# Conditioning slices of a diffusion block: every slice that is worked out beside other stages goes to VectorE alone, and weight splits stand between pairs of chunks at three layer entries

## The chip, the cores and the metric

The kernel runs on one core of one Trainium2 chip. The metric is the device time in microseconds of one execution; the number quoted for the kernel is the median of several runs.

## The reference

The program is a backbone of four layers (D = 1024) over 256 latent tokens (`x`) and 256 context tokens (`ctx`). Each layer is a token mixer (neighbourhood attention in layers 0 and 3, retention in layer 1, a Conformer convolution module in layer 2) and a convolutional gated feed-forward part. Every one of these eight parts is preceded by an RMS norm whose result is scaled and shifted, and followed by a gated residual; shift, scale and gate come from a conditioning vector, another one for latent than for context tokens:

```python
silu_c, silu_cc = jax.nn.silu(c), jax.nn.silu(c_ctx)[None, :]
for i in range(DEPTH):
    mx = jnp.split((silu_c @ ada_w[i] + ada_b[i])[:, None, :], 6, axis=-1)    # 1024 x 6144 weights
    mc = jnp.split((silu_cc @ ada_w[i] + ada_b[i])[:, None, :], 6, axis=-1)
    hx = rms_norm(xs, norm_mix[i]) * (1 + mx[1]) + mx[0]
    hc = rms_norm(cs, norm_mix[i]) * (1 + mc[1]) + mc[0]
    yx, yc = mixer(hx, hc)                       # attention, retention or convolution
    xs = xs + mx[2] * yx
    hx = rms_norm(xs, norm_ffn[i]) * (1 + mx[4]) + mx[3]
    u, v = jnp.split(hx @ w_up, 2, axis=-1)      # 1024 x 5632
    u = jax.nn.gelu(depthwise_conv(u, w_dw, b_dw))
    xs = xs + mx[5] * ((u * v) @ w_down)         # 2816 x 1024
    # cs the same with mc, except in the last layer
```

## The kernel before, in words

**The large products.** The residual stream `X` lies in SBUF as 8 chunks of 128 features by 512 tokens (256 context, called CT, and 256 latent, called XT). All weights are streamed from memory in 424 groups of 128 x 1024 float32 into four slots (`raw`). To multiply at near float32 precision each group is split: ScalarE rounds it to a high half `Whi` (L1266) and VectorE subtracts that from the raw weights to get the low half `Wlo` (L1680). The activations are split alike into `Hhi` (ScalarE) and `Hlo` (VectorE), and TensorE forms three products for each pair: high by high, low by high, high by low (L748 to L750; L754 to L756 where the tokens stand on the partitions). One group is 24 such products of 512 columns. `split(st)` on both engines splits the group three (`LEAD`) ahead of `st`.

**The order** is written out by hand: each engine has its own program, and semaphores tie them together. `weights_used` counts the groups that TensorE is done with, `lo_split` the split ones, `tile_free` the output tiles that were taken from PSUM, `h_ready` the normed chunks.

**Conditioning.** The 6144 outputs of a layer's conditioning matrix are 48 slices of 128; apart from the first 16, each is a weight block of 128 x 1024 (`cond_w`, three slots, loaded by DMAs that ScalarE issues) that has to be multiplied by each of the two conditioning vectors (`cond`, rows 0 and 1) and summed along its 1024 columns. This is not done on TensorE. It is *hosted*: slices are put between VectorE's instructions of other stages. `weigh(n)` on VectorE is a product with a sum in one instruction (L1704), and `cond_store(n)` (L1715) adds the bias three slices later. For some slices VectorE does both vectors. For the others, which are `shared(n)`, VectorE does the product with row 1, then GpSimd multiplies the block in place by row 0 (`scale_weights`, L608), and ScalarE sums the result (`sum_products`, L1283), after which `reload` fetches the next block. Shared are 12 slices in the q, k and v products of layer 0 (`HOSTED`: so many slices in each quarter of each of six blocks of output columns) and all 99 slices of the feed-forward up-projections of layers 0 to 2, which run 11 laps of four groups with three slices a lap. Six slices (`IN_OUT`) are hosted in the output projection of layer 0, one after each tile, the rest in the down-projections.

**Between parts.** Before each norm the squares of `X` have to be summed: GpSimd does it chunk by chunk as tiles of the residual come (`after_residual`, L600 and L602), ScalarE squares the last chunk, and TensorE sums over the features (`norm_sum`). To have TensorE work meanwhile, the last tiles of a projection are made in halves: first their context half, then the latent half, with the norm of the context half in between (`last_halves`, `norm_halves`). The next part then begins with three tiles together, chunk by chunk as these become ready (`three_tiles`; in layer 3 `by_streams`). At such an entry VectorE scales chunks (L1765), makes their low halves (L1756) and splits the next two or three weight groups, called `following`.

**The convolution module** computes a gate per chunk (ScalarE a sigmoid, L1538, VectorE the product `U`, L2107). 31 taps are then shared among VectorE, ScalarE with GpSimd, and TensorE; TensorE's part (L1161) needs shifted copies of `U`, made by DMAs once `U` is there.

## Time and profile before

| | us |
|---|---|
| median of 3 runs | 2446.84 (2445.07 to 2448.78) |
| the profiled execution | 2448.26 |
| its span, from the first to the last instruction | 2446.1 |
| TensorE (PE) busy in it | 2381.3 |
| VectorE (DVE) busy | 1782.1 |
| ScalarE (ACT) busy | 1025.6 |
| GpSimd (POOL) busy | 657.2 |
| mean granted TensorE clock | 0.993 of full speed |

Busy time is the time in which an engine has an instruction in it. TensorE's instructions overlap, so a busy TensorE can still be paced by something; where it stands still the timeline shows the length of the wait in brackets, with the instruction that ended it.

### The profile page before, as it was taken

How to read it: one execution, taken by the hardware profiler on the slowest of the kernel's cores; microseconds unless marked ns; L12 is line 12 of the kernel's file. 1: busy time of each engine (PE TensorE's matmuls, PEld its weight loads, DVE VectorE, ACT ScalarE, POOL GpSimd, SP SyncE). 2: the span in 40 equal slices, each digit the busy share in tenths (PEclk: the TensorE clock that was granted, in tenths of full speed). 3: DMA queues.
4: the chain of work that ended last, by engine and by line, in shares of the span. 5: the costliest groups of instructions: out<-in, count | busy, mean ns of one | idle time of the engine just before them, and what ended most of it. 6: DMA issues, size and time to landing. Idle time of an engine off the chain costs nothing. (4 is left out here: it accounts for less than half of the span.)

```text
span 2446.1 us, 35542 instructions
## 1 busy us (share of the span) xinstructions
PE 2381.3 (97%) x12398; PEld 1951.9 (80%) x12398; DVE 1782.1 (73%) x2667; ACT 1025.6 (42%) x1557; POOL 657.2 (27%) x445
## 2 busy tenths in 40 slices
PE   8998999999999999999999999999999999998999
PEld 6874688888888878888888888668888887867999
DVE  5777788888974355428988777988988775556774
ACT  4356434443232334314444325554444323555543
POOL 2553433333200030022333225843333224101000
PEclk9999999999999999999999999999999999999999
DMA  8550235446633311223555544523554545312556
GB/s 301 166 187 1 70 117 178 163 160 215 207 101 110 99 67 61 95 95 138 171 175 174 178 152 124 148 79 138 172 174 160 185 159 136 122 44 74 190 184 190
DMA packets 104648, 346.20 MB, mean 142 GB/s; under 512 B 13232, under 2 KB 22896, under 8 KB 104544
## 3 DMA queue, kind: packets, MB, share of 16 engines
q1 hardware_dynamic: 72656, 240.26, 29.4%
q10 hardware_dynamic: 28656, 95.16, 12.0%
q0 software_dynamic: 3232, 9.38, 1.8%
q8 instruction: 68, 1.11, 0.2%
q14 instruction: 36, 0.29, 0.0%
HBM read 334.96 MB, written 1.05 MB: 137 GB/s over the span
## 5 line engine op out<-in xcount | busy, mean ns | idle before, releaser
L1680 DVE TENSOR_TENSOR Wlo<-raw,Whi 128x1024 fp32r<-128x1024 f32 x424 | 637.5, 1504 | 268.6 <-ACT Whi L1266 264.9
L1266 ACT ACTIVATE Whi<-raw 128x1024 fp32r<-128x1024 f32 x424 | 448.4, 1060 | 810.0 <-DMA raw<-in_weights 712.7
L748 PE MATMUL bank<-Hhi,Whi 128*128 128x512 f32 (+1 forms) x2136 | 763.3, 357 | 12.5 <-DVE Hlo L1756 5.4
L749 PE MATMUL bank<-Hlo,Whi 128*128 128x512 f32 (+1 forms) x2136 | 755.8, 354 | 0.0
L750 PE MATMUL bank<-Hhi,Wlo 128*128 128x512 f32 (+1 forms) x2136 | 755.7, 354 | 0.0
L748 PEld LDWEIGHTS bank<-Hhi,Whi 128*128 128x128 f32 x2136 | 404.7, 189 | 78.0 <-issue 12.6
L750 PEld LDWEIGHTS bank<-Hhi,Wlo 128*128 128x128 f32 x2136 | 404.7, 189 | 55.3
L749 PEld LDWEIGHTS bank<-Hlo,Whi 128*128 128x128 f32 x2136 | 404.8, 190 | 55.0
L608 POOL TENSOR_TENSOR cond_w<-cond_w,cond 128x1024 f32<-128x1024 f32 x111 | 270.3, 2435 | 556.8 <-DVE square L1704 510.9
L748 PE MATMUL bank<-Ghi,Whi 128*128 128x512 f32 (+1 forms) x770 | 268.3, 348 | 0.9 <-DVE Wlo L1680 0.9
L749 PE MATMUL bank<-Glo,Whi 128*128 128x512 f32 (+1 forms) x770 | 267.3, 347 | 0.0
L750 PE MATMUL bank<-Ghi,Wlo 128*128 128x512 f32 (+1 forms) x770 | 267.2, 347 | 0.0
L600 POOL TENSOR_TENSOR square<-X 128x512 f32<-128x512 f32 (+1 forms) x51 | 76.7, 1503 | 462.9 <-DVE X L1850 453.0
L1704 DVE SCALAR_TENSOR_TENSOR hb<-cond_w,cond 128x1024 f32<-128x1024 f32 x142 | 196.7, 1385 | 4.8
L754 PE MATMUL bank<-Whi,Hhi 128*128 128x512 f32 x480 | 190.1, 396 | 5.8 <-DVE Wlo L1680 2.3
L756 PE MATMUL bank<-Wlo,Hhi 128*128 128x512 f32 x480 | 188.2, 392 | 0.0
L755 PE MATMUL bank<-Whi,Hlo 128*128 128x512 f32 x480 | 188.1, 392 | 0.0
L748 PEld LDWEIGHTS bank<-Ghi,Whi 128*128 128x128 f32 x770 | 144.3, 187 | 22.8 <-DVE Wlo L1680 0.6
L749 PEld LDWEIGHTS bank<-Glo,Whi 128*128 128x128 f32 x770 | 144.3, 187 | 21.6
L750 PEld LDWEIGHTS bank<-Ghi,Wlo 128*128 128x128 f32 x770 | 144.3, 187 | 21.4
L1604 ACT ACTIVATE hb<-hb 128x512 f32<-128x512 f32 (+1 forms) x88 | 51.0, 579 | 216.7 <-DVE hb L2255 216.7
L1283 ACT ACTIVATE cond_w<-cond_w 128x1024 f32<-128x1024 f32 x111 | 116.7, 1052 | 48.0 <-POOL cond_w L608 41.6
(278 smaller groups left out, 2871.0 us busy)
## 6 DMA issues: line engine op xcount, KB each, us to landing
raw<-in_weights SPq DMA_DIRECT2D x424, 512.0 KB, 3.4
cond_w<-in_ada ACTq DMA_DIRECT2D x176, 512.0 KB, 4.1
ada_raw<-in_ada SPq DMA_DIRECT2D x16, 512.0 KB, 15.0
rel_in<-in_rpb POOLq DMA_DIRECT2D x48, 128.0 KB, 5.8
shifted<-U SPq DMA_DIRECT2D x84, 66.0 KB, 2.1
decay_t<-in_dist POOLq DMA_DIRECT2D x4, 640.0 KB, 4.2
X<-in_x SPq DMA_DIRECT2D x4, 512.0 KB, 5.9
shifted<-U ACTq DMA_DIRECT2D x28, 66.0 KB, 2.1
```

Source lines behind the costliest of these rows:

```text
L600: g.tensor_tensor(square[:, c % 2, tok], X[:, c, tok], X[:, c, tok], ALU.mult).then_inc(sum_step, 1)
L608: g.tensor_tensor(w, w, cond[:, 0, :], ALU.mult).then_inc(cond_scaled, 1)
L748: t.matmul(dst, Whi[:, st.slot, w], hi, start=start, stop=False)
L749: t.matmul(dst, Whi[:, st.slot, w], lo, start=False, stop=False)
L750: return t.matmul(dst, Wlo[:, st.slot, w], hi, start=False, stop=stop)
L754: t.matmul(dst, hi, Whi[:, st.slot, w], start=start, stop=False)
L755: t.matmul(dst, lo, Whi[:, st.slot, w], start=False, stop=False)
L756: return t.matmul(dst, hi, Wlo[:, st.slot, w], start=False, stop=stop)
L1266: a.activation(Whi[:, st.slot, :], raw[:, st.slot, :], ACT.Copy).then_inc(hi_split, 1)
L1283: a.activation(w, w, ACT.Copy, accum_out=cond_sum[:, n % COND_SLOTS, 0:1]).then_inc(cond_summed, 1)
L1680: v.tensor_tensor(Wlo[:, st.slot, :], raw[:, st.slot, :], Whi[:, st.slot, :].bitcast(F32), ALU.subtract)\
L1704: last = v.scalar_tensor_tensor(scratch, w, 1.0, cond[:, r, :], ALU.mult, ALU.mult, accum_out=cond_sum[:, slot, r:r + 1])
```

## The change

- `shared` is gone. VectorE does both products of every slice; GpSimd's product and ScalarE's sum are removed, and `reload` waits for VectorE alone.
- `HOSTED` goes from 18 to 20 slices in the q, k and v products of layer 0 and `IN_OUT` from 6 to 4.
- Entries into layers 1 and 2: VectorE scales chunks 2 and 3 before it splits a weight group, and makes their low halves after it; TensorE begins with the products of chunks 0 and 1 for the first tile alone, before it waits for the group of the second (`early`). Entry into layer 3: each of three groups is split after one pair of chunks.
- Convolution: the sigmoid and the gate of chunk 1 are moved to the end of chunk 0.
- At the start of the program ScalarE makes the high half of chunk 2 before that of a weight group.

```diff
-HOSTED = ((0, 0, 0, 0), (0, 1, 1, 1), (1, 1, 1, 0), (1, 1, 1, 1), (1, 1, 1, 1), (1, 1, 1, 1))
+HOSTED = ((0, 0, 0, 0), (0, 1, 1, 1), (1, 1, 1, 1), (1, 1, 1, 1), (1, 1, 1, 1), (2, 1, 2, 0))
-IN_OUT = 6
+IN_OUT = 4
...
         def weighed(n):
-            return 2 * (n + 1) - shared_before(n + 1)
+            return 2 * (n + 1)
...
-            def scale_weights(n, per=0, i=0):
-
-                pool.wait_ge(cond_weighed, weighed(n) + per * i)
-                w = cond_w[:, n % COND_SLOTS, :]
-                g.tensor_tensor(w, w, cond[:, 0, :], ALU.mult).then_inc(cond_scaled, 1)
...
                 pe.wait_ge(tile_free, index + 2)
+                early = 2 if r % 2 == 0 else 0
+                for k in range(early):
+                    pe.wait_ge(h_ready, ready + k + 1)
+                    three(bank[0][:, CT], steps[0], slice(P * k, P * k + P), Hhi[:, k, CT], Hlo[:, k, CT], k == 0, False)
                 pe.wait_ge(lo_split, steps[1].n + 1)
                 for k in range(C):
                     pe.wait_ge(h_ready, ready + k + 1)
-                    for m in range(2):
+                    for m in range(1 if k < early else 0, 2):
...
-            def sum_products(n, per=0, i=0):
-
-                nth = shared_before(n)
-                act.wait_ge(cond_scaled, nth + 1 + per * i)
-                w = cond_w[:, n % COND_SLOTS, :]
-                a.activation(w, w, ACT.Copy, accum_out=cond_sum[:, n % COND_SLOTS, 0:1]).then_inc(cond_summed, 1)
...
                 square_last(r, XT)
-                high(r, 0, 4, 6)
-                split(following[1])
+                if r == 2 * DEPTH - 2:
+                    split(following[1])
+                    high(r, 0, 4, 6)
+                    split(following[2])
+                else:
+                    high(r, 0, 4, 6)
+                    split(following[1])
                 high(r, 0, 6, C)
...
                     for n, tap in enumerate(pool_taps[c]):
+                        if c == 0 and n == 5:
+                            sigmoid(1)
...
+            first_high(2)
             split(Step(2 - LEAD))
-            first_high(2)
...
-                for q, r in enumerate((1,) if shared(n) else (0, 1)):
+                for q, r in enumerate((0, 1)):
                     if first + q:
-                        dve.wait_ge(cond_weighed, first + q + per * i)
+                        dve.wait_ge(cond_weighed, first + q + 2 * per * i)
...
-                    if c > first:
+                    if c > first and between is None:
                         low(c - 1)
+                if between is not None:
+                    split(between)
+                    low(end - 2)
                 low(end - 1)
...
-                if r % 2 == 0:
+                if r == 2 * DEPTH - 2:
                     split(following[0])
-                    normed_chunks(r, 0, 2, 4)
+                elif r % 2 == 0:
+                    normed_chunks(r, 0, 2, 4, following[0])
...
-                    if c == C - 2:
-                        gate(C - 1)
+                    if c in (0, C - 2):
+                        gate(c + 1)
```

What stands where, word for word, at three places (line numbers are those of each version). First VectorE in the last block of v columns of layer 0, up to the copies of v (`COPY V`); before:

```order
92 L1680 TENSOR_TENSOR Wlo<-raw,Whi 128x1024
93 L1715 TENSOR_TENSOR mod<-cond_sum,bias_ada 128x2
94 L1704 SCALAR_TENSOR_TENSOR hb,cond_sum<-cond_w,cond 128x1024
95 L1680 TENSOR_TENSOR Wlo<-raw,Whi 128x1024
96 L1715 TENSOR_TENSOR mod<-cond_sum,bias_ada 128x2
97 L1704 SCALAR_TENSOR_TENSOR hb,cond_sum<-cond_w,cond 128x1024
98 L1715 TENSOR_TENSOR mod<-cond_sum,bias_ada 128x2
99 L1704 SCALAR_TENSOR_TENSOR hb,cond_sum<-cond_w,cond 128x1024
100 L1715 TENSOR_TENSOR mod<-cond_sum,bias_ada 128x2
101 L1704 SCALAR_TENSOR_TENSOR hb,cond_sum<-cond_w,cond 128x1024
102 L1904 COPY V<-bank 128x512 x2
```

and after:

```order
94 L1656 TENSOR_TENSOR Wlo<-raw,Whi 128x1024
95 L1689 TENSOR_TENSOR mod<-cond_sum,bias_ada 128x2
96 L1680 SCALAR_TENSOR_TENSOR hb,cond_sum<-cond_w,cond 128x1024 x2
97 L1689 TENSOR_TENSOR mod<-cond_sum,bias_ada 128x2
98 L1680 SCALAR_TENSOR_TENSOR hb,cond_sum<-cond_w,cond 128x1024 x2
99 L1656 TENSOR_TENSOR Wlo<-raw,Whi 128x1024
100 L1689 TENSOR_TENSOR mod<-cond_sum,bias_ada 128x2
101 L1680 SCALAR_TENSOR_TENSOR hb,cond_sum<-cond_w,cond 128x1024 x2
102 L1689 TENSOR_TENSOR mod<-cond_sum,bias_ada 128x2
103 L1680 SCALAR_TENSOR_TENSOR hb,cond_sum<-cond_w,cond 128x1024 x2
104 L1689 TENSOR_TENSOR mod<-cond_sum,bias_ada 128x2
105 L1680 SCALAR_TENSOR_TENSOR hb,cond_sum<-cond_w,cond 128x1024 x2
```

Four slices with one product each have become five with two, ten products instead of four.

Then VectorE at the end of the output projection of layer 0, from the fifth tile's residual (`X<-bank,mod,X`) to the halves of the last two tiles; before:

```order
283 L1850 SCALAR_TENSOR_TENSOR X<-bank,mod,X 128x256 x2
284 L1680 TENSOR_TENSOR Wlo<-raw,Whi 128x1024
285 L1715 TENSOR_TENSOR mod<-cond_sum,bias_ada 128x2
286 L1704 SCALAR_TENSOR_TENSOR hb,cond_sum<-cond_w,cond 128x1024 x2
287 L1850 SCALAR_TENSOR_TENSOR X<-bank,mod,X 128x256 x2
288 L1680 TENSOR_TENSOR Wlo<-raw,Whi 128x1024
289 L1715 TENSOR_TENSOR mod<-cond_sum,bias_ada 128x2
290 L1704 SCALAR_TENSOR_TENSOR hb,cond_sum<-cond_w,cond 128x1024 x2
291 L1715 TENSOR_TENSOR mod<-cond_sum,bias_ada 128x2 x3
292 L1842 SCALAR_TENSOR_TENSOR X<-bank,mod,X 128x256 x2
```

and after:

```order
287 L1832 SCALAR_TENSOR_TENSOR X<-bank,mod,X 128x256 x2
288 L1656 TENSOR_TENSOR Wlo<-raw,Whi 128x1024
289 L1832 SCALAR_TENSOR_TENSOR X<-bank,mod,X 128x256 x2
290 L1656 TENSOR_TENSOR Wlo<-raw,Whi 128x1024
291 L1689 TENSOR_TENSOR mod<-cond_sum,bias_ada 128x2 x3
292 L1824 SCALAR_TENSOR_TENSOR X<-bank,mod,X 128x256 x2
```

Two slices, each a store and two products, are gone from between the tiles.

Last VectorE at the entry into layer 1, from the scaling of the first two chunks (`hb<-X,scale,bank`); before:

```order
479 L1765 SCALAR_TENSOR_TENSOR hb<-X,scale,bank 128x256 x2
480 L1756 SCALAR_TENSOR_TENSOR Hlo<-hb,mod,Hhi 128x256 x2
481 L1680 TENSOR_TENSOR Wlo<-raw,Whi 128x1024
482 L1765 SCALAR_TENSOR_TENSOR square<-X,scale,bank 128x256 x2
483 L1756 SCALAR_TENSOR_TENSOR Hlo<-square,mod,Hhi 128x256 x2
```

and after:

```order
488 L1739 SCALAR_TENSOR_TENSOR hb<-X,scale,bank 128x256 x2
489 L1730 SCALAR_TENSOR_TENSOR Hlo<-hb,mod,Hhi 128x256 x2
490 L1739 SCALAR_TENSOR_TENSOR square<-X,scale,bank 128x256 x2
491 L1656 TENSOR_TENSOR Wlo<-raw,Whi 128x1024
492 L1730 SCALAR_TENSOR_TENSOR Hlo<-square,mod,Hhi 128x256 x2
```

The scaling of chunks 2 and 3 has moved ahead of the split.

## Rows read from the trace of the kernel before

**Rows 1.** The page's busy table: busy us, share of the span, instructions.
```profile
PE 2381.3 (97%) x12398; PEld 1951.9 (80%) x12398; DVE 1782.1 (73%) x2667; ACT 1025.6 (42%) x1557; POOL 657.2 (27%) x445
```

**Rows 2.** VectorE by line, 350 to 560 us, then 2260 to 2375; busy, mean | idle before.
```profile
L1680 DVE TENSOR_TENSOR Wlo<-raw,Whi 128x1024 fp32r<-128x1024 f32 x40 | 78.8, 1971 | 4.6 <-ACT Whi L1266 4.6
L1704 DVE SCALAR_TENSOR_TENSOR square<-cond_w,cond 128x1024 f32<-128x1024 f32 x30 | 36.7, 1224 | 1.9
...
L1680 DVE TENSOR_TENSOR Wlo<-raw,Whi 128x1024 fp32r<-128x1024 f32 x40 | 48.8, 1221 | 17.0 <-ACT Whi L1266 17.0
```

**Rows 3.** Timeline of a lap in layer 0, VectorE and GpSimd: start, us, instruction [wait].
```profile
490.65 0.81 DVE L2250 TENSOR_SCALAR hb<-bank,fff 128x512 f32<-128x512 f32 x1 [1.63 <-PE bank L750]
...
496.37 3.01 DVE L1680 TENSOR_TENSOR Wlo<-raw,Whi 128x1024 fp32r<-128x1024 f32 x1
...
501.51 0.81 DVE L2250 TENSOR_SCALAR hb<-bank,fff 128x512 f32<-128x512 f32 x1 [0.19 <-issue]
...
495.89 2.40 POOL L608 TENSOR_TENSOR cond_w<-cond_w,cond 128x1024 f32<-128x1024 f32 x1 [8.57 <-DVE square L1704]
```

**Rows 4.** Timeline of VectorE in layer 0, a slice that it does alone.
```profile
100.12 0.15 DVE L1715 TENSOR_TENSOR mod<-cond_sum,bias_ada 128x2 f32<-128x2 f32 x1
100.31 1.23 DVE L1704 SCALAR_TENSOR_TENSOR hb<-cond_w,cond 128x1024 f32<-128x1024 f32 x1
...
101.57 1.23 DVE L1704 SCALAR_TENSOR_TENSOR hb<-cond_w,cond 128x1024 f32<-128x1024 f32 x1
```

**Rows 5.** VectorE by line, 107.7 to 173.8 us; then the timeline, VectorE and TensorE.
```profile
L1704 DVE SCALAR_TENSOR_TENSOR hb<-cond_w,cond 128x1024 f32<-128x1024 f32 x12 | 19.1, 1593 | 0.4
L1680 DVE TENSOR_TENSOR Wlo<-raw,Whi 128x1024 fp32r<-128x1024 f32 x11 | 15.6, 1417 | 8.6 <-ACT Whi L1266 8.6
L1715 DVE TENSOR_TENSOR mod<-cond_sum,bias_ada 128x2 f32<-128x2 f32 x12 | 10.6, 885 | 0.0
...
173.70 1.28 DVE L1904 COPY V<-bank 128x512 f32<-128x512 f32 x2
...
175.47 1.23 PE L1013 MATMUL bank<-QK 64*128 64x256 f32 x4 [2.58 <-DVEq L1906]
```

**Rows 6.** Stretches: length, busy PE, PEld, DVE, ACT, POOL; clock; DMA share, GB/s.
```profile
171.40:186.00 14.60, 11.57 (x56) 6.91 (x55) 8.69 (x21) 7.30 (x19) 7.28 (x6) 0.77 0.47 142
315.20:333.60 18.40, 12.80 (x75) 12.32 (x74) 13.30 (x30) 5.76 (x12) 5.15 (x6) 0.72 0.28 90
1663.90:1674.60 10.70, 9.36 (x76) 9.00 (x76) 9.38 (x22) 4.50 (x10) 1.44 (x3) 1.00 0.32 100
```

**Rows 7.** Timeline at the end of layer 0's output projection, VectorE and TensorE.
```profile
318.99 0.86 DVE L1842 SCALAR_TENSOR_TENSOR X<-bank,mod,X 128x256 f32<-128x256 f32 x2
...
321.01 1.02 PE L858 MATMUL bank<-one,total 128*128 128x2 f32 x4 [5.60 <-POOL total L602]
```

**Rows 8.** Timeline at the entries into layers 1, 2 and 3.
```profile
696.76 0.35 PE L748 MATMUL bank<-Hhi,Whi 128*128 128x256 f32 x1 [0.70 <-issue]
...
1483.67 0.87 DVE L1765 SCALAR_TENSOR_TENSOR square<-X,scale,bank 128x256 f32<-128x256 f32 x2
...
1483.85 0.36 PE L748 MATMUL bank<-Hhi,Whi 128*128 128x256 f32 x1 [1.53 <-issue]
...
2045.65 0.73 PE L754 MATMUL bank<-Whi,Hhi 128*128 128x512 f32 x1 [2.27 <-DVE Wlo L1680]
...
2055.79 0.58 PE L754 MATMUL bank<-Whi,Hhi 128*128 128x512 f32 x1 [1.90 <-DVE Hlo L1756]
```

**Rows 9.** Timeline at the start of layer 2's up-projection, TensorE and VectorE.
```profile
1695.85 0.50 PE L748 MATMUL bank<-Hhi,Whi 128*128 128x512 f32 x1 [0.66 <-DVE Wlo L1680]
...
1699.75 1.36 DVE L1680 TENSOR_TENSOR Wlo<-raw,Whi 128x1024 fp32r<-128x1024 f32 x1
```

**Rows 10.** Timeline of TensorE in the convolution, at chunk 1's taps.
```profile
1524.34 2.78 PE L1161 MATMUL bank<-shifted,taps_diagonal 128*32 128x512 f32 x24 [1.81 <-DMA shifted<-U]
```

More of the change, by code:

```diff
@@ L80 @@
 PER_LAP = 3
-HOSTED = ((0, 0, 0, 0), (0, 1, 1, 1), (1, 1, 1, 0), (1, 1, 1, 1), (1, 1, 1, 1), (1, 1, 1, 1))
+HOSTED = ((0, 0, 0, 0), (0, 1, 1, 1), (1, 1, 1, 1), (1, 1, 1, 1), (1, 1, 1, 1), (2, 1, 2, 0))
 IN_SLICES = sum(map(sum, HOSTED))
-IN_OUT = 6
+IN_OUT = 4
 IN_MIX = IN_SLICES + IN_OUT
-ALONE = sum(HOSTED[1]) + sum(HOSTED[2])
 V_LATE = 2
@@ L470, in streams @@
             return 2 if tok == ALL else 1
-        def shared(n):
-            return ALONE <= n < IN_SLICES or any(p["hosts"] and p["cond_up"] <= n < p["cond_down"] for p in layers)
-        def shared_before(n):
-            return sum(shared(q) for q in range(n))
         def weighed(n):
-            return 2 * (n + 1) - shared_before(n + 1)
+            return 2 * (n + 1)
         def in_down(layer, group):
@@ L649, in pairs_staged @@
                 pool.wait_ge(rel_ready, 2 * j + 2)
-                if layer == 0:
-                    pool.wait_ge(cond_ready, 2)
-                    for n in range(ALONE, IN_SLICES):
-                        scale_weights(n)
                 h = Heads(layer)
@@ L728, in _ @@
                 after_residual(r + 1, out_tile, norm_tokens(layer, 1))
-                if p["hosts"]:
-                    with pool.Fori(0, FC // 2) as i:
-                        for q in range(PER_LAP):
-                            scale_weights(p["cond_up"] + q, PER_LAP, i)
                 if layer < DEPTH - 1:
@@ L1339, in norm_apply @@
                 square_last(r, XT)
-                high(r, 0, 4, 6)
-                split(following[1])
+                if r == 2 * DEPTH - 2:
[5 more added lines that the diff above has]
+                    split(following[1])
                 high(r, 0, 6, C)
-                for st in following[2:]:
-                    split(st)
                 root_of_norm(r, XT)
@@ L1416, in na @@
                 if layer == 0:
-                    sum_products(IN_SLICES - 1)
                     reload(IN_SLICES - 1, p["cond_end"])
@@ L1531, in conv, with sigmoid @@
                 act.wait_ge(cos_loaded, 32)
+                def sigmoid(c):
+                    act.wait_ge(weights_used, p["mix"] + 2 * c + 2)
+                    a.activation(glu_s[:, c % 2, :], bank[2 * (c % 2) + 1][:, :], ACT.Sigmoid,
+                                 bias=cvb[:, 1, c:c + 1]).then_inc(glu_sigmoid, 1)
                 for c in range(C):
@@ L1536, in conv @@
                         split(steps[0])
-                    act.wait_ge(weights_used, steps[1].n + 1)
-                    a.activation(glu_s[:, k, :], bank[2 * k + 1][:, :], ACT.Sigmoid,
-                                 bias=cvb[:, 1, c:c + 1]).then_inc(glu_sigmoid, 1)
+                    if c != 1:
+                        sigmoid(c)
                     if c == C - 1:
@@ L1711, in cond_store @@
                 earlier = 2 * MODS if k + per >= 2 * MODS else 0
-                dve.wait_ge(cond_weighed, weighed(n) + per * i)
-                if shared(n):
-                    dve.wait_ge(cond_summed, shared_before(n) + 1 + per * i)
+                dve.wait_ge(cond_weighed, weighed(n) + 2 * per * i)
                 v.tensor_tensor(mod_slices[:, bass.ds(k - earlier + per * i, 1), :], cond_sum[:, slot:slot + 1, :],
@@ L1745, in norm_scale, with normed_chunks @@
                 dve.wait_ge(scale_ready, r + 1)
-            def normed_chunks(r, half, first, end):
+            def normed_chunks(r, half, first, end, between=None):
                 layer, part = r // 2, r % 2
@@ L1827, in norm_halves @@
                 normed_chunks(r, 0, 0, 4 if r % 2 else 2)
-                if r % 2 == 0:
+                if r == 2 * DEPTH - 2:
                     split(following[0])
-                    normed_chunks(r, 0, 2, 4)
+                elif r % 2 == 0:
+                    normed_chunks(r, 0, 2, 4, following[0])
                 dve.wait_ge(weights_used, following[1].n + 1)
                 add_half(tiles[-1], bank[6], 1, XT, tile_free)
-                normed_chunks(r, 0, 4, C)
-                split(following[1])
-                for st in following[2:]:
-                    split(st)
+                if r == 2 * DEPTH - 2:
+                    for n in range(1, 4):
+                        normed_chunks(r, 0, 2 * n, 2 * n + 2)
+                        if n < 3:
+                            split(following[n])
+                else:
+                    normed_chunks(r, 0, 4, C)
+                    split(following[1])
                 invert_root(r, XT)
@@ L2114, in conv @@
                         split(steps[0])
-                    gate(c)
+                    if c != 1:
+                        gate(c)
+                    else:
+                        dve.wait_ge(tap_done, taps_before[c])
                     dve.wait_ge(tile_free, FREE0 + p["mix_tile"] + 2 * c + 1)
```

10 lines of the change are left out of this document (1 added, 9 removed).

## The prediction, made before the changed kernel ran

> **What bounds the kernel now.** The page's busy table comes first: TensorE is busy 2381.3 us of a span of 2446.1, so all of its idle time together is 64.8 us, and VectorE is the next engine with 1782.1 [rows 1]. A change to VectorE's work can then do two things: it can become the bound inside a loop, or it can lengthen or shorten one of the few places where TensorE stands still. So the second view is VectorE in time, in a lap of the feed-forward up-projection, and the third is the list of TensorE's stalls in the timeline.
>
> In the up-projection TensorE doesn't wait at all once the loop runs. A lap is four weight tiles. VectorE starts on the output of one at 490.65 and on that of the second next at 501.51, so two take 10.86 us, one 5.43 and a lap 21.7; and once per lap it waits for TensorE, 1.63 us at 490.65 [rows 3]. That wait (and 0.2 of small ones) is the room which VectorE has per lap: about 1.8 us. The grouped rows say what fills the rest: in 210 us, which is 40 weight tiles or 10 laps, 40 low halves take 78.8 us at 1971 ns, and 30 hosted products 36.7 us at 1224 ns. In the last layer, where GpSimd does nothing, the same low half takes 1221 ns [rows 2]. The timeline shows why: GpSimd's product starts at 495.89 and lasts 2.40, to 498.29; the low half that starts at 496.37 lasts 3.01, to 499.38, which is 1.1 after GpSimd is done [rows 3]. The reader is to see that VectorE doesn't run slower beside GpSimd, it stands still until GpSimd's instruction has ended.
>
> **The up-projections (3 x 11 laps).** Removed per lap: three GpSimd products and three ScalarE sums, none on the path. Added: three more VectorE products. What a second product costs is seen in a slice that VectorE does alone: starts at 100.31 and 101.57, so 1.26 us [rows 4]; 3 x 1.26 = 3.8 us a lap. Given back: the low halves, 4 x (1.971 - 1.221) = 3.0 us a lap [rows 2]. Net +0.8 us against 1.8 of room, so VectorE keeps 1.0 us a lap and the loop stays TensorE's: 0 us. If the blocking did not go away, the lap would be 3.8 - 1.8 = 2.0 us longer.
>
> The first lap is different, since VectorE starts it late and has no room yet. In layer 2 TensorE gets its tile at 1695.85 after 0.66 of waiting, and wants the next 5.44 later, at 1701.3; that low half starts at 1699.75 and ends at 1701.1 [rows 9]. One more product stands ahead of it (+1.26; -0.14 of blocking goes), so TensorE waits about 0.9. Layer 1 has the same picture, layer 0 a little more slack: 2 x 0.8 = +1.6 us. From both sides: 0 (a blocked low half of the first lap becomes free) to 3 x 1.26 = 3.8.
>
> That exchange can be read in the Trainium skill too. SBUF — State Buffer, in its section on the two sides, says that VectorE (with two SBUF inputs) and GpSimd share a port pair as an exclusive lock, held for a whole instruction: by that rule the blocking goes entirely with the GpSimd products, and the trace agrees (3.01 against 1.22 us). Perfetto Trace Analysis, under Optimizing Scalar/DVE Operations, says that with a saturated VectorE it may make sense to hand work to other engines; by that alone the added 3.8 us a lap would all be a loss, 33 x 2.0 = 66 us. It is the first rival below.
>
> **The q, k and v products of layer 0.** Twelve slices get a second product (12 x 1.26 = 15.1 us) and two slices move here from the output projection; one takes a store and two products, 0.19 + 2 x 1.26 = 2.7 us [rows 4], so 5.4: +20.5 us on VectorE before the attention starts. Back come the blocked instructions. The store of a finished slice, two columns wide, takes 0.15 us alone [rows 4], but the 12 stores between 107.7 and 173.8 take 10.6 us, so 8.8 of it is blocking. The 12 products there take 19.1 instead of 12 x 1.224 = 14.7 (4.4 us), and the 11 low halves 1417 instead of 1221 ns (2.2 us) [rows 5]. ScalarE's sums also wait for GpSimd and hold back its next high half, for which VectorE waits 8.6 us in all [rows 5]; 7.4 of it should go. Together 22.8, so VectorE ends its slices 2.3 us before its present 173.70, near 171.4, which is about when TensorE's last v product ends. One thing gets later: the third block of columns now hosts four slices, which delays the rows of that block by one slice's 2.7 us; I bound the wait that this gives from 0 to 2.7 and take 0.2, since the rows now come well before TensorE turns them (no wait for them stands there). Now TensorE waits 2.58 us for the copies of v behind that queue, until 175.47 [rows 5]; of this I take back 2.5. The wait is followed by a stretch with a mean granted clock of 0.77 [rows 6]; 14.6 us x 0.23 is 3.4 us lost at most, and as most of the work there is a chain through other engines I take 1.5. Sum -4.0 us, roundly (bounds +1, if VectorE is later rather than earlier, and -6).
>
> **The output projection of layer 0.** This is the largest term. Six slices are hosted there, one a tile, each with instructions blocked by GpSimd's squares, so VectorE falls behind: it adds the first halves of the last tiles only at 318.99, after the last slice; GpSimd's squares follow, and TensorE waits 5.60 us, to 321.01, for the sum of squares [rows 7]. The clock falls too: the stretch 315.2 to 333.6 has a mean of 0.72, while the same stretch in layer 2, which hosts nothing, has 1.00 and takes 10.7 us instead of 18.4 [rows 6]. After the change the last two tiles host nothing, which takes 5.4 us and their blocking from VectorE just before this point; the four earlier slices meet the same blocking as now. VectorE is then waiting for TensorE by the seventh tile. Gain: 18.4 - 10.7 = 7.7, less 0.2 for a rest of GpSimd's lag: -7.5 us (bounds -3 and -8).
>
> **The entries into layers 1, 2 and 3.** TensorE waits there for one low half (0.70 and 1.53 us), and in layer 3 for another (2.27) and for a normed chunk (1.90) [rows 8]. The change puts two scaled chunks (0.87 us [rows 8]) ahead of a low half for which VectorE stands waiting, and gives TensorE six half products before it needs that half. Worth the 0.9 and a little in layer 2, where VectorE really waits: -1.0; -0.7 in layer 1, where the low half itself comes 0.3 later. In layer 3 the third weight tile is split before chunks 4 and 5 instead of after 7, so the 2.27 shrinks to about 1 and the chain behind it moves up; but GpSimd's additions for the bias table there don't move, and block the normed chunks as before: -2.5. Sum -4.2 (bounds -1 and -6).
>
> **The convolution.** The second gate is computed a few microseconds earlier, so that its shifted copies are there when TensorE asks for them; now it waits 1.81 us [rows 10]. But VectorE and ScalarE pace this stage and TensorE would mostly wait a little later instead: -0.3 (bounds 0 and -1.8). The swapped pair on ScalarE at the start of the program is put at nothing: TensorE's next chunks there wait for weights that are still being loaded, and if that cover were gone it is worth under 1 us.
>
> **Sum.** +1.6 - 4.0 - 7.5 - 4.2 - 0.3 = -14.4 us. The profiled execution took 2448.26 (span 2446.1), 1.4 above the median of 2446.84; so 2433.9 for a like execution, 2432.4 for the median.
>
> **Rivals.**
> - VectorE becomes the bound in the up-projections (slower). Place: each of the 33 laps. It decides once the net addition passes the 1.8 us of room. With the full 3.8 it costs 2.0 x 33 = 66 us: 2498. Half of the blocking left (1.5 us a lap more) costs 0.5 x 33 = 16 and eats the gains: 2449. Against it speak the 1221 ns of the last layer and the exact ends beside GpSimd. Chance 0.06.
> - A new wait takes the place of the one in the output projection: GpSimd's own queue of squares is still late, half of the 5.60 stays and the clock falls all the same. Then that term is -3.5 and the time 2436.5. Chance 0.17.
> - VectorE ends the v stage no earlier, and TensorE waits for rows besides: the term of layer 0's attention start is +1 instead of -4: 2437.5. Chance 0.15. With the previous one together, and little at the entries, it is 2443, within the measurement: chance 0.08.
> - The granted clock holds better than I take it for, at all three places: another 4 us, 2428. Chance 0.10.
> - The forecast as it stands: 0.44.
>
> **Numbers.** The range is 2427 to 2441: it holds the forecast, the clock case and the two single rivals, and leaves out the VectorE bound and the sum of failures. About 0.2% (4.9 us) is what a measurement of this kernel can tell from no change. Faster by more: 0.44 + 0.10 + 0.17 + 0.15 = 0.86; within: 0.08 and half of the first rival rounded, 0.09; slower: 0.05.
>
> **What would show it.** In the changed profile the low halves of layers 0 to 2's up-projections should have a mean near 1.22 us, the hosted products twice the number at the same 1.22, and VectorE should still wait about 1 us a lap for TensorE. The wait for GpSimd's sum in layer 0 should be gone and the stretch there near 11 us at a clock of 1; the wait before the attention under 0.5. In layers 1 and 2 one or two waits of about 1 us for a low half stand at the start of the up-projection. The prediction is wrong if TensorE waits for low halves in every lap, or if the 7.5 us come back as a later wait.

## The result, and the profile after

The changed kernel takes 2433.04 us, the median of 4 runs (2429.46 to 2437.48), against 2447.62 for the kernel before (4 runs on the same chip). The ratio is 0.9941, with a 95% interval of 0.9927 to 0.9956, so it is faster by 11 to 18 us. The profiled execution is the fastest of the four: 2429.46, with a span of 2427.6, which is 18.5 below the 2446.1 of before. The 4 us between this trace and the median matter below.

The busy table of the changed kernel, which answers to [rows 1] (busy us, share, instructions):

```profile
PE 2372.9 (98%) x12398; PEld 1944.3 (80%) x12398; DVE 1795.1 (74%) x2889; ACT 906.2 (37%) x1335; POOL 383.2 (16%) x334
```

GpSimd has lost 274 us of work and ScalarE 119, while VectorE, which took over both, has gained only 13. The 111 products that it does more (12 + 99) would be 140 us at 1.26; the rest was time in which it stood blocked (its 424 low halves alone fell from 637.5 to 535.4 us). VectorE by line in the up-projection of layer 0, 340 to 550 us, in answer to [rows 2] (busy, mean ns of one | idle before):

```profile
L1680 DVE SCALAR_TENSOR_TENSOR square<-cond_w,cond 128x1024 f32<-128x1024 f32 x60 | 73.5, 1225 | 4.6
L1656 DVE TENSOR_TENSOR Wlo<-raw,Whi 128x1024 fp32r<-128x1024 f32 x40 | 48.7, 1217 | 0.0
```

Sixty products instead of thirty at the same 1.22 us, and the forty low halves have gone from 1971 to 1217 ns. VectorE's starts on the outputs of a lap, with its wait in brackets, in answer to [rows 3]:

```profile
478.16 0.81 DVE L2235 TENSOR_SCALAR hb<-bank,fff 128x512 f32<-128x512 f32 x1 [1.57 <-PE bank L726]
...
489.56 0.81 DVE L2235 TENSOR_SCALAR hb<-bank,fff 128x512 f32<-128x512 f32 x1
...
499.92 0.81 DVE L2235 TENSOR_SCALAR hb<-bank,fff 128x512 f32<-128x512 f32 x1 [1.57 <-PE bank L726]
```

A lap is still 21.76 us, and VectorE still waits for TensorE once in it. The two stretches of layer 0 that [rows 6] showed at clocks of 0.77 and 0.72 (length, busy PE, PEld, DVE, ACT, POOL; clock; DMA share, GB/s):

```profile
171.40:186.00 14.60, 14.06 (x89) 8.75 (x88) 10.43 (x33) 8.21 (x26) 4.49 (x5) 1.00 0.27 98
...
310.50:321.10 10.60, 9.37 (x75) 8.96 (x74) 7.69 (x20) 4.47 (x10) 1.99 (x3) 1.00 0.30 100
```

Both have the full clock. In the first TensorE hardly stops; the second holds the same 75 matmuls that took 18.40 us before and takes 10.60, like the stretch of layer 2 in [rows 6] (10.70). At the end of the output projection, where it waited 5.60 us for GpSimd's sum [rows 7], the timeline now has

```profile
311.18 0.61 PE L838 MATMUL bank<-one,total 128*128 128x2 f32 x4 [0.53 <-POOL total L592]
```

**Where the time went, stage by stage.** Both programs give TensorE the same 12398 matmuls in the same order (but for a few at the entries), so two traces can be laid side by side: for the matmul of the same number, start after minus start before; the growth of that difference in a stage is what the stage gained or lost. The table does so for the main kernels of this study, in us against the trace of before. The columns: from the program's start to 97 us (the second block of q); the attention start of layer 0 (171 to 185); its output projection's end (311 to 334); the entries into layers 1 (689 to 709), 2 (1477 to 1493) and 3 (2041 to 2087); the first laps of the up-projections of layers 1 and 2; the convolution (1493 to 1626); what follows 2087. The first two rows are two executions of one program: they differ by 4.2 in the first column, 2.3 in the last, 1.0 in the convolution and 0.8 in the first "up1", and by 0.3 at most elsewhere.

```text
kernel               start  attn  outproj  L1    up1   L2    conv  up2   L3    rest
changed              +1.2  -5.9   -7.8   -0.8  +1.3  -1.7  +0.1  +1.1  -4.4  -1.7
changed, again       +5.4  -5.9   -7.8   -0.8  +0.5  -1.4  +1.1  +1.1  -4.4  +0.6
hosting only         +0.8  -5.9   -7.8    0.0  +0.9  -0.3  +0.1  +1.0  -1.2  +1.5
orders only          +5.9  -5.2   -0.5   -0.8   0.0  -1.4  +0.2   0.0  -4.4  -0.5
old spread           +5.6  -5.9   -0.2   -0.8  +1.5  -1.3  -0.5  +1.0  -4.4  -1.7
spread only          +1.1  +5.8   -7.8    0.0   0.0  -0.2  +0.6  +0.1  -3.6  -1.7
up shared            +0.6  -5.9   -7.8   -0.8  +0.1  -1.6  +0.2  -0.2  -4.4  -0.5
slice earlier        -1.2  -5.9   -7.8   -0.8  +0.6  -1.7  -0.5  +1.3  -4.4  +0.3
```

Three columns can be trusted, since they repeat to a tenth of a microsecond: the attention start in the six rows with the hosting (-5.9), the output projection in the six with the new spread (-7.8), the entry into layer 1 in the six with the new orders (-0.8). The first column isn't, and no edit was expected to show there. Nor is the last, where no edit is: it goes from -1.7 to +1.5. Part of it is the clock. Behind the same 2.13 us wait at the entry into the last feed-forward part the clock falls to half in five of the fourteen traces ("changed, again", at 2244.1 us, is one) and not in the others, which costs 1.0 to 1.3 us; the rest comes in the last 60 us of the program.

### The profile page after: what moved, and what is told of

Read it like the earlier page. It is cut to its first block and busy times, and to the rows that moved or that the text cites. A ratio compares the mean times of both kernels' runs of the same rounds, so it can differ in the third digit from the quotient of the medians.

```text
span 2427.6 us, 35365 instructions
## 1 busy us (share of the span) xinstructions
PE 2372.9 (98%) x12398; PEld 1944.3 (80%) x12398; DVE 1795.1 (74%) x2889; ACT 906.2 (37%) x1335; POOL 383.2 (16%) x334
## 5 line engine op out<-in xcount | busy, mean ns | idle before, releaser
L1656 DVE TENSOR_TENSOR Wlo<-raw,Whi 128x1024 fp32r<-128x1024 f32 x424 | 535.4, 1263 | 244.3 <-ACT Whi L1246 240.4
L1680 DVE SCALAR_TENSOR_TENSOR square<-cond_w,cond 128x1024 f32<-128x1024 f32 x198 | 242.5, 1225 | 14.9
L1680 DVE SCALAR_TENSOR_TENSOR hb<-cond_w,cond 128x1024 f32<-128x1024 f32 x154 | 202.7, 1316 | 5.2
L730 PEld LDWEIGHTS bank<-Whi,Hhi 128*128 128x128 f32 x480 | 90.1, 188 | 28.4 <-issue 5.7
```

Of the source, the lines that this page charges most:

```text
L730: t.matmul(dst, hi, Whi[:, st.slot, w], start=start, stop=False)
L1656: v.tensor_tensor(Wlo[:, st.slot, :], raw[:, st.slot, :], Whi[:, st.slot, :].bitcast(F32), ALU.subtract)\
L1680: last = v.scalar_tensor_tensor(scratch, w, 1.0, cond[:, r, :], ALU.mult, ALU.mult, accum_out=cond_sum[:, slot, r:r + 1])
```

## The experiments

Each was compared with the kernel before on the same chip, where that one had medians of 2445.77, 2449.18 and 2448.09 us on the three chips that were used. So ratios are given, and what they come to in us is counted with 2447.

### The parts alone: hosting, and orders

The hosting alone is the changed kernel with these pieces put back as they were:

```diff
-                early = 2 if r % 2 == 0 else 0
-                for k in range(early):
...
+            split(Step(2 - LEAD))
             first_high(2)
-            split(Step(2 - LEAD))
```

and likewise in `norm_halves`, `normed_chunks` and the convolution.

> The changed kernel with the old orders at the layer entries, in the convolution and at the start of the program; the conditioning is hosted on VectorE alone with the new spread (20 and 4 slices). My theory: the terms of the hosting stand alone, +1.6 (first laps of the up-projections) -4.0 (attention start of layer 0) -7.5 (output projection of layer 0) = -9.9 us against the kernel before; from the profile of the changed kernel, which gave +1.2 at the start of two up-projections each, -5.9 at the attention start and -7.8, rather -11. Rival: the new orders and the hosting help each other (a low half that comes earlier at an entry only since GpSimd doesn't block it), then this kernel keeps less than -8 and the orders alone give less than -3.

Measured: 2436.63 us (5 runs), ratio 0.9958, interval 0.9945 to 0.9972: -10 us. The orders alone are the kernel before with just these pieces:

> The kernel before with the new orders alone (three layer entries, convolution, start of the program); conditioning shared with GpSimd and ScalarE as before. My theory: -4.2 at the entries and -0.3 in the convolution, -4.5 us. Rival: the orders only pay with the hosting changed, 0 to -2. Other rival: they are worth more than I gave them, since the changed kernel's milestones fall by 0.8, 1.5 and 4.1 us at the three entries: -6.

Measured: 2440.93 us, ratio 0.9980, interval 0.9970 to 0.9989: -5 us. The two add up to -15, the whole change has -14.5, so the times show no dependence between the parts. Each interval is 5 to 7 us wide, so one of a few us could hide in them. In the table "hosting only" has the three large terms and "orders only" those of the entries. But the latter shows +5.9 before 97 us and then -5.2 at the attention start, where nothing of it is; both are taken up below.

### The spread of the slices alone, and everything but the spread

```diff
-HOSTED = ((0, 0, 0, 0), (0, 1, 1, 1), (1, 1, 1, 1), (1, 1, 1, 1), (1, 1, 1, 1), (2, 1, 2, 0))
+HOSTED = ((0, 0, 0, 0), (0, 1, 1, 1), (1, 1, 1, 0), (1, 1, 1, 1), (1, 1, 1, 1), (1, 1, 1, 1))
-IN_OUT = 4
+IN_OUT = 6
```

> The changed kernel with the old spread of slices: 18 in the q, k and v products, 6 in the output projection of layer 0, all on VectorE alone. My theory: it is the two slices at the end of the output projection that hold VectorE back, so the 5.6 us wait of TensorE for GpSimd's sum of squares returns with a clock below 0.8 in that stretch, and the kernel is 6 to 7.5 us slower than the changed one (-7 to -8.5 us against before). Rival: VectorE comes out of the attention earlier without GpSimd's products and catches up by itself; then the wait stays under 1 us and the time is that of the changed kernel within 1 us.

Measured: 2441.9 us, ratio 0.9983, interval 0.9974 to 0.9993: -4 us, so 10 worse than the changed kernel, where 6 to 7.5 was expected. TensorE's wait is back (5.61 us, before 5.60), and the clock falls with it, to 0.81 where below 0.8 was expected:

```profile
320.69 1.02 PE L838 MATMUL bank<-one,total 128*128 128x2 f32 x4 [5.61 <-POOL total L592]
...
314.90:333.00 18.10, 11.79 (x74) 11.29 (x73) 13.20 (x29) 5.68 (x11) 5.14 (x6) 0.81 0.27 90
```

The first line is from the timeline of this kernel, the second from its windows. The table's output projection is at -0.2 instead of -7.8: it is the two slices and nothing else, and the rival (VectorE catches up by itself) falls. The remaining 2 to 3 us of the difference lie in the start column, which has +5.6 here.

The other way round, the kernel before with the new spread alone:

> The kernel before with the new spread alone (20 slices in the q, k and v products, 4 in the output projection), shared with GpSimd and ScalarE as before. My theory: the output projection gains its 7.5 us, as the slices there were VectorE's alone anyway, but two more shared slices in the last block of v (each a blocked store of 0.9, a product of 1.6 and the sum behind GpSimd) make TensorE's wait for the copies of v 4 to 5 us longer: sum -3 us. Rival: the v stage swallows them, -7.5.

Measured: 2443.93 us, ratio 0.9990, interval 0.9979 to 1.0000: -2 us where -3 was expected, at the edge of what can be told from none. The output projection gives -7.8 and the attention start takes 5.8 back, since TensorE now waits there for the copies of v behind GpSimd's products:

```profile
181.43 1.22 PE L1013 MATMUL bank<-QK 64*128 64x256 f32 x4 [6.98 <-DVEq L1906]
```

So the move of the two slices needs VectorE's freedom from GpSimd, and that is the real coupling in this change: alone it gives back 5.8 of the 7.8 us that it wins. The hosting without it keeps its 5.9 at the attention start ("old spread").

### Does GpSimd block VectorE, and how much room has a lap?

GpSimd gets its products back in the 33 laps, on data of its own, so that nothing depends on them:

```diff
+                            g.tensor_tensor(spare, cond[:, 0, :].rearrange("p (a t) -> p a t", a=2), cond[:, 1, :].rearrange("p (a t) -> p a t", a=2), ALU.mult).then_inc(beside, 1)
```

> The changed kernel, and beside each of the three slices of a lap of the up-projections of layers 0 to 2 GpSimd makes a product of 128x1024 again (99 in all), of the two conditioning vectors into memory that nobody reads; it is added work, nothing waits for it but the end of the up-projection. My theory: VectorE stands still while GpSimd multiplies, about 3.0 us a lap as in the kernel before (low halves of 1971 ns), which with VectorE's own 7.6 us of products passes its room: (3.0 - 1.0) x 33 = 66 us slower than the changed kernel; at least +45 if more of GpSimd's time falls on VectorE's instructions that read PSUM. Rival: the long low halves of before came from the memory traffic or from ScalarE's sums, which aren't here; then low halves keep 1.22 us and the time stays within 5 us.

Measured: 2512.88 us, ratio 1.0262, interval 1.0246 to 1.0278: 64 above the kernel before and 78 above the changed one. VectorE and GpSimd in the timeline of a lap, then VectorE by line from 340 to 550 us:

```profile
500.42 3.12 DVE L1671 TENSOR_TENSOR Wlo<-raw,Whi 128x1024 fp32r<-128x1024 f32 x1
506.58 1.22 DVE L1671 TENSOR_TENSOR Wlo<-raw,Whi 128x1024 fp32r<-128x1024 f32 x1
...
500.06 2.40 POOL L720 TENSOR_TENSOR spare_all<-cond 128x1024 f32<-128x1024 f32 x1 [3.96 <-DVE square L1695]
...
L1671 DVE TENSOR_TENSOR Wlo<-raw,Whi 128x1024 fp32r<-128x1024 f32 x35 | 77.3, 2209 | 0.0
```

GpSimd's product ends at 502.46 and the low half begun at 500.42 ends at 503.54, 1.08 later; the next, with GpSimd idle, takes 1.22. ScalarE's sums are absent here, and the loads are those of the changed kernel, where the low halves take 1217 ns; so the rival that blamed the sums or the traffic falls. The Trainium skill, in SBUF — State Buffer, section on the two sides, says that the pair is locked for a whole instruction, and this run agrees by adding one engine's work and nothing else. A lap is 23.93 us, 2.17 more (24.04 in layer 1), and 33 laps make some 72 of the 78 us (the span is 76.4 longer than that of "changed, again"); this is the first rival's mechanism (66 us), which exists, and which the change avoids since it takes GpSimd's products away.

Then VectorE alone gets more work, one product a lap and two (on the constants, written to the same scratch). This is the second run; the first has `(3,)` for `(1, 3)`, and the lines left out are waits:

```diff
+                        if p["hosts"] and m in (1, 3):
...
+                            v.scalar_tensor_tensor(square[:, :, :].rearrange("p k t -> p (k t)"), cond[:, 0, :], 1.0, cond[:, 1, :],
+                                                   ALU.mult, ALU.mult, accum_out=spare_sum[:, 0:1]).then_inc(beside, 1)
```

> The changed kernel with one more product of 128x1024 on VectorE in each of the 33 laps (1.26 us, added work that nobody reads). It measures the room. By the prediction's room of 1.0 us a lap: (1.26 - 1.0) x 33 = +9 us. By the wait that the changed kernel's own trace shows for VectorE in a lap, 1.57 us: 0, apart from one or two us in the first laps of layers 1 and 2, +2. Rival, VectorE is already the bound of the loop: +42.

> The changed kernel with two more products on VectorE in each of the 33 laps (2.52 us). By a room of 1.0 us a lap: 1.52 x 33 = +50 us. By a room of 1.6: +30. Rival, no room: +83.

Measured: one more is 2438.27 us (ratio 0.9959, 0.9943 to 0.9974), 4 above the changed kernel; two more 2464.27 (1.0066, 1.0050 to 1.0083), 31 above it. The laps say it better than the times: with one more a lap is 21.76 us exactly as before, with two it is 22.41. VectorE's own lap is then 22.41, and 2 x 1.25 less than that, 19.9, without the additions: the room in the changed kernel is 1.85 us a lap. With one more, VectorE's starts in the timeline are 21.24 us apart in layer 0 while TensorE's laps are 21.76, since it is still catching up after a late start; that gives 0.52 + 1.25 = 1.77. The forecast had left 1.0. Against the changed kernel's second execution ("changed, again"), the spans differ by 0.9 us with one more (2435.6 and 2434.7), with the start column alike, and by 25.4 with two (2460.1), with the start 1.0 less: 33 x 0.65 = 21, and some 5 in first laps. By the ratios the two are 4 and 31 us above the changed kernel, since its first measurement was the faster one; see below.

### The up-projections shared again

The changed kernel, but with `shared(n)` kept for the 99 slices of the up-projections:

```diff
+        def shared(n):
+            return any(p["hosts"] and p["cond_up"] <= n < p["cond_down"] for p in layers)
```

> The changed kernel with the up-projections alone as before: their 99 slices shared with GpSimd and ScalarE again; the mixer part of layer 0 stays on VectorE alone with the new spread and the new orders. My theory: the 33 laps are TensorE's either way, and the added product costs only in the first laps of layers 1 and 2, so this kernel is 1 to 2 us faster than the changed one (-16 us against before). Rival: taking GpSimd's products out of the up-projections is itself a gain that the sum missed (a stage of 680 us with a blocked VectorE); then this kernel is 2 us or more slower than the changed one.

Measured: 2433.21 us, ratio 0.9940, interval 0.9926 to 0.9954; the changed kernel has 0.9941. In time that is no difference. In the traces the two columns of the first laps are at +0.1 and -0.2 instead of +1.3 and +1.1, as the theory has it. So in the 33 laps the exchange of GpSimd and ScalarE for VectorE brings nothing; by the traces it costs 1.7 to 2.5 us in first laps, which the times can't tell. What it brings lies in the mixer part of layer 0 alone.

### The start

The first column of the table was not foreseen, so the changed kernel ran again as the level for the next ones.

> The changed kernel once more, as the level for the next three on the same chip, and to see how much its start varies: at about 93 us TensorE waited for the normed rows of q (line qk_rows) 2.3 us in one execution and 4.1 to 4.3 in three other kernels whose program up to there is the same or nearly so. My theory: whether GpSimd's bias rows (rel) come in time to block VectorE's products there is set by the moment at which two loads land, so the wait differs from execution to execution, 2 to 4.5 us. Rival: the order of ScalarE's first instructions sets it, then this kernel shows 2.3 again.

Measured: 2436.54 us (5 runs), ratio 0.9950, interval 0.9937 to 0.9964. Its trace has the longer wait. VectorE, GpSimd and TensorE in it, from 80 to 97 us, and the window around:

```profile
83.86 10.68 POOL L629 TENSOR_TENSOR rel<-rel_in,mask 128x384 f32<-128x384 f32 x8 [9.76 <-DMA rel_in<-in_rpb]
...
85.87 2.02 DVE L1680 SCALAR_TENSOR_TENSOR hb<-cond_w,cond 128x1024 f32<-128x1024 f32 x1
...
87.94 1.91 DVE L1680 SCALAR_TENSOR_TENSOR hb<-cond_w,cond 128x1024 f32<-128x1024 f32 x1
...
95.71 3.67 PE L920 MATMUL bank<-ident,qk_rows 128*128 128x128 f32 x16 [4.27 <-DVE qk_rows L1879]
...
92.00:100.00 8.00, 4.29 (x18) 4.13 (x19) 7.51 (x13) 2.41 (x4) 2.54 (x3) 0.61 0.22 66
```

and the same rows of the kernel before:

```profile
88.28 9.69 POOL L645 TENSOR_TENSOR rel<-rel_in,mask 128x384 f32<-128x384 f32 x8 [10.18 <-DMA rel_in<-in_rpb]
...
84.22 1.22 DVE L1704 SCALAR_TENSOR_TENSOR hb<-cond_w,cond 128x1024 f32<-128x1024 f32 x1
85.48 1.22 DVE L1704 SCALAR_TENSOR_TENSOR hb<-cond_w,cond 128x1024 f32<-128x1024 f32 x1
...
92.57 1.97 PE L940 MATMUL bank<-ident,qk_rows 128*128 128x128 f32 x16 [1.25 <-DVE qk_rows L1897]
```

GpSimd makes the bias rows (`rel`) of the attention when their loads have landed. Before, this begins at 88.28, after VectorE's two products of a hosted slice; here at 83.86, ahead of them, and the products take 2.02 and 1.91 instead of 1.22 each. VectorE's normed rows of q come later by that, TensorE waits 4.27 us instead of 1.25, and the clock falls (0.61 from 92 to 100 us, 1.00 in the trace of before): the sixteen short matmuls take 3.67 us instead of 1.97. Together 5 us.

What sets the moment? In the three traces without the new order of ScalarE's first instructions (before, hosting only, spread only) `rel` begins at 88.28, 89.18 and 87.26, and both products take 1.22 or 1.23. In the eleven traces with it, it begins at 83.2 to 86.2; nine of them have the products there. In seven both are blocked, and these are 3.9 to 6.1 us behind the trace of before at 97 us. In the first trace of the changed kernel only the second one is blocked (+1.2), and they are free in the one with `rel` at 86.23 ("up shared", +0.6). The three without the edit have 0 to 1.1.

The chain in front of it moves as well: GpSimd's first loads of the bias table start at 42.16 to 42.39 without and at 40.81 to 41.83 with the edit, since TensorE's conditioning products before them are 1.2 us earlier (39.62 and 38.43 in the traces of before and of this one). On the way this grows: the second set of these loads is issued at 68.58 to 69.93 without and at 65.41 to 68.10 with the edit.

Up to 93 us "hosting only" and the changed kernel differ in that edit alone. So the cheapest looking edit, put at nothing, makes GpSimd about 1 us earlier at the start and TensorE some 4.5 us later in most traces. It was not run by itself, so that it is the edit, and not the executions that happened to be traced, rests on this count (seven of nine, none of three), and what it costs the median is an inference: "hosting only", without it and without the entries' 3 to 7 us, is 2 us behind the changed kernel's second measurement and 4 behind its first (ratios 0.9958, 0.9950 and 0.9941).

### Two ways to mend it

The first moves one slice on VectorE from behind a low half that it waits 8 us for to ahead of it:

```diff
-                        for n in hosted_in(y, quarter):
+                        slices = {(1, 2): (1, 2), (1, 3): ()}.get((y, quarter), hosted_in(y, quarter))
+                        for n in slices:
                             weigh(n, scratch, follows=n >= COND_SLOTS)
```

> The changed kernel with VectorE's products of the third slice moved from behind the low half of the last group before the head norms of the second q block (where TensorE waits for it 2 to 4 us) to ahead of it, where VectorE waits 8 us for that group. Theory: two products of 1.23 us leave the path to the normed rows (2.5 us, up to 4 where GpSimd's rel blocks them), the clock doesn't fall there either: -2.5 to -4 us against the changed kernel. But VectorE still ends the v stage only just in time, so if TensorE waits there for the copies of v, the gain is partly given back: rival, -1 or less.

Measured: 2429.25 us (2428.11 to 2431.19), ratio 0.9926, interval 0.9912 to 0.9940: 7.3 below the changed kernel on the same chip, more than expected. The timeline of VectorE and TensorE:

```profile
75.56 1.23 DVE L1680 SCALAR_TENSOR_TENSOR hb<-cond_w,cond 128x1024 f32<-128x1024 f32 x1
...
76.82 1.23 DVE L1680 SCALAR_TENSOR_TENSOR hb<-cond_w,cond 128x1024 f32<-128x1024 f32 x1
...
84.14 1.36 DVE L1656 TENSOR_TENSOR Wlo<-raw,Whi 128x1024 fp32r<-128x1024 f32 x1 [6.08 <-ACT Whi L1246]
...
91.36 1.97 PE L920 MATMUL bank<-ident,qk_rows 128*128 128x128 f32 x16
```

No wait is left, although `rel` begins at 83.41 here: there is nothing for it to block. The gain is the whole start column, +5.4 to -1.2, and none of it is given back before the attention (-5.9 as ever). This is the best kernel of the study, 18 us below the kernel before. Its runs lie within 3 us, those of the changed kernel on this chip within 5.

The second puts the three slices of the first lap in layers 1 and 2 one tile later:

```diff
-                        if p["hosts"] and m < PER_LAP:
-                            weigh(p["cond_up"] + m, ...)
+                        q = m - 1 if first and layer else m
+                        if p["hosts"] and 0 <= q < PER_LAP:
+                            weigh(p["cond_up"] + q, ...)
```

> The changed kernel with the three slices of the first lap of the up-projections in layers 1 and 2 each one weight tile later, so that the low halves of the first two tiles come ahead of them. Theory: the two waits of 0.7 us for a low half at each of these starts go, 2 x 1.4 = -2.8 us, as the lap has 1.6 us of room afterwards. Rival: the products delay the next low halves instead, the waits move to the end of the first lap: 0.

> Both of the two edits before together. Theory: they are 1000 us apart and add up, -5 to -7 us against the changed kernel, about -20 us against the kernel before. Rival: the first is swallowed before the attention, -3.

Measured: the deferral alone 2436.25 us (0.9954, 0.9941 to 0.9968), 0.3 below the changed kernel; both 2430.17 (0.9929, 0.9915 to 0.9942), no better than the first alone. The deferral is worth nothing. TensorE's waits at the start of layer 1's up-projection with the deferral, and ScalarE's high half in front:

```profile
1129.78 0.50 PE L724 MATMUL bank<-Hhi,Whi 128*128 128x512 f32 x1 [0.50 <-DVE Wlo L1656]
1136.23 0.50 PE L724 MATMUL bank<-Hhi,Whi 128*128 128x512 f32 x1 [0.69 <-DVE Wlo L1656]
...
1127.41 1.06 ACT L1246 ACTIVATE Whi<-raw 128x1024 fp32r<-128x1024 f32 x1 [1.79 <-DMA raw<-in_weights]
```

The first wait is for a weight load that has just landed, so it doesn't matter what VectorE does meanwhile; the second is for a low half that still has a product, deferred to that place, ahead of it.

## Why the prediction was right, and where it was not

The forecast was 2432.4 us and the time is 2433.0, by terms that were not all right.

- **The loop of the up-projections: 0, confirmed.** The lap is 21.76 us in both. The net addition to VectorE was put at 0.8 us a lap, yet its wait for TensorE only went from 1.63 to 1.57. The term that was off is what came back. Ten laps of it (217.6 us from 350 and from 338 us) have 191.90 us of busy time before and 196.62 after, so +0.47 a lap; and its waits for ScalarE's high halves, 4.6 us in ten laps before [rows 2], are 0.0 after. The forecast had counted the low halves rightly (0.75 us each) and left these waits out. The room is 1.77 to 1.85 us.
- **First laps: +1.6 forecast, +2.4 in the trace** (1.3 and 1.1), +1.6 in the second one, and 0 with the slices shared. Right in kind: two waits of 0.7 in each of the two layers, where one of 0.41 and 0.66 was.
- **Attention start: -4.0 forecast, -5.9 measured.** The account of VectorE's queue held: it ends its slices at 171.6 (forecast 171.4) and waits 1.19 us for TensorE before the last copies of v. The wait of 2.58 is gone in full. The term that was too small is the clock: 1.5 was taken, 3.3 is what it gives, nearly all of the 3.4 that the stretch at 0.77 held by multiplication. That the work there is a chain through other engines was no reason to halve it. "Orders only" shows the same from the other side: its TensorE comes 5.9 late to this place, VectorE's queue doesn't, no wait is left, and the -5.2 are the same wait and the same clock. So in the kernel before about 5 us of delay in the q products were free, and after the change they are not; this is why the start column only hurts now.
- **Output projection: -7.5 forecast, -7.8 measured** in every trace with the new spread, and about 0 in the two without. The comparison with layer 2's same stretch (18.4 against 10.7 us) was the right way to size it. The rival of a late GpSimd is there with 0.53 us.
- **Entries: -0.7, -1.0 and -2.5 forecast; -0.8, -1.3 to -1.7 and -4.4 measured.** Of the last, not all is the change's: the trace of before has a low clock there (two stretches in 2045 to 2060), while "spread only", with the same program there, has none and is 3.6 faster at that place too. The windows of 2030 to 2080 us of before, and of "spread only":

```profile
2030.00:2080.00 50.00, 45.83 (x218) 37.77 (x217) 31.26 (x48) 18.30 (x31) 25.39 (x33) 0.93 0.65 147
```

```profile
2030.00:2080.00 50.00, 45.25 (x226) 36.89 (x225) 35.51 (x55) 19.62 (x34) 26.56 (x34) 1.00 0.66 152
```

  With the new order the clock was 1.00 in that stretch in all eleven traces. What the order is worth lies between 0.8 (against "spread only") and 4.4, and more can't be told from three traces of the old one.
- **Convolution: -0.3 forecast, no gain seen** (-0.5 to +1.1 in the rows with the edit, 0.1 and 0.6 in the two without). The 1.81 us wait for shifted copies is gone, and TensorE waits 2.23 for a low half 11 us later instead of 0.58, as the forecast said it would:

```profile
1519.76 0.77 PE L724 MATMUL bank<-Hhi,Whi 128*128 128x512 f32 x1 [2.23 <-DVE Wlo L1656]
```

- **The swap at the start: 0 forecast, +4 to +6 in seven of nine traces.** This is the step that failed. It asked only what TensorE waits for next, and stopped there; it did not follow GpSimd, whose transfers begin when TensorE is done with the conditioning and whose products then block VectorE 45 us later. The profile of before had all of it: the `rel` products at 88.28, 1.6 us behind the last hosted product before the normed rows.

The errors cancel: some +4.5 at the start in a usual execution, against 1.9 more at the attention and up to 1.9 more at the entry into layer 3. The total was right partly by luck. For the profiled execution the forecast was 2433.9 us, and it took 2429.46; 1.7 of that stand in the last column, which no edit made. In the chances, "within" adds up to 0.11 (0.08 and half of 0.06) and not 0.09. The profiled execution of the changed kernel was one of the two with a short wait at the start (+1.2), which can be why it lies 4 us below the median.

## What to carry to other kernels

VectorE got nearly all the work that it had handed to GpSimd back as blocked time: it took over 111 products and had 13 us more of busy time. So compare the total of an engine with and without the help. Size a removed wait by the same stage where it doesn't occur, clock included: a wait of 2.6 us was worth 5.9, one of 5.6 was worth 7.8. And when an edit makes anything earlier, follow what that triggers on the engines that share something, and put movable work in front of a wait, not behind it, even where it costs nothing today.

## What the hardware showed that was not expected

- The granted clock doesn't follow from the wait alone. A wait of 2.27 us at the same matmul (entry into layer 3) was followed by half clock in the trace of before, and the same wait of 2.28 us by full clock in that of "spread only". The 2.13 us wait before the last feed-forward part was followed by half clock in five of fourteen traces.
- Small shifts grow. In the eleven traces with the new order at the start GpSimd's `rel`, which waits for a load, begins anywhere from 83.24 to 86.23 us, and VectorE's last low half ahead of the products from 83.57 to 85.03; a blocked pair of products, a wait of 3.6 to 5.0 us and the clock make 4 to 6 us of that. The changed kernel's runs differ by 8 us, those of the kernel without anything to block ("slice earlier") by 3; but the kernel before spreads as far (2442.6 to 2451.4 in 27 runs), and what moves it was not traced.
- VectorE isn't blocked by GpSimd in every instruction: in the trace with GpSimd's added products the instructions of VectorE that read PSUM keep their lengths (`hb<-bank,fff` 802 ns from 400 to 600 us, against 808 in the changed kernel), and one addition (`hb<-bank,fff,hb`) takes its usual 0.75 us at 518.34, wholly inside a product of GpSimd's that lasts from 517.63 to 520.04. The low halves, with both inputs in SBUF, grow from 1217 to 2209 ns in the mean.
